# Mixer units 2 to 6 as products of 512 columns over four PSUM banks going round

## The reference, cut to what matters

```python
def short_conv_mixer(h, w_in, conv_w, w_out):
    bg, cg, v = jnp.split(h @ w_in, 3, axis=-1)
    return (bg * causal_dwconv(cg * v, conv_w)) @ w_out
...
x = x + short_conv_mixer(rmsnorm(x, mix_norm[layer]), a_w_in[i], a_conv[i], a_w_out[i])
```

## Time and profile before

| | |
|---|---|
| median of 3 runs | 619.44 us (619.2 to 619.78) |
| the profiled execution's own time | 619.53 us |
| its span, from first to last instruction | 617.8 us |
| TensorE busy | 604.2 us, 98% of the span |
| VectorE busy | 482.2 us, 78% |
| ScalarE busy | 390.6 us, 63% |
| mean granted clock of TensorE | 0.997 |

### The profile page before, as it was taken

The page is one execution under the profiler, slowest core; times in us unless marked ns, Lnnn a source line. Parts: engine busy times, 40 slices in busy tenths (PEclk is TensorE's granted clock), DMA queues, the critical chain, the costliest instruction groups (busy, mean ns, idle before and its releaser), DMA issues.

```text
span 617.8 us, 11378 instructions
## 1 busy us (share of the span) xinstructions
PE 604.2 (98%) x3764; PEld 530.5 (86%) x3764; DVE 482.2 (78%) x955; ACT 390.6 (63%) x727; POOL 57.5 (9%) x81
## 2 busy tenths in 40 slices
PE   9999999999999999999999999999999999999995
PEld 8999997988888888887989877778988888888884
DVE  4888656788888887886877899938788888888765
ACT  7546336766666666667657598737766666666644
POOL 0100011000000000003110156600100000000010
PEclk9999999999999999999999999999999999999998
DMA  8797432355555655781467401023465655555521
GB/s 331 297 342 245 172 136 102 127 214 203 198 198 203 199 199 199 264 288 58 134 205 238 154 2 36 15 94 133 134 213 206 200 194 204 201 191 202 196 102 68
DMA packets 30352, 109.55 MB, mean 177 GB/s; under 512 B 3387, under 2 KB 3659, under 8 KB 30188
## 3 DMA queue, kind: packets, MB, share of 16 engines
q1 hardware_dynamic: 29756, 106.97, 49.4%
q0 software_dynamic: 560, 2.12, 1.0%
HBM read 108.01 MB, written 1.07 MB: 177 GB/s over the span
## 4 chain that ended last, share of the span: by engine, by line
PE 90%; DVE 4%; ACT 2%; issue 1%; DMA 1%; POOL 0%; SPq 0%; DVEq 0%; ACTq 0%
PE bank L1260 24%; PE bank L1264 12%; PE bank L1209 10%; PE bank L1210 10%; PE bank L1211 10%; PE bank L1228 10%; PE bank L1233 5%; PE bank L1305 2%; PE bank L1318 1%; PE bank L1598 1%; DMA bias<-in_xT 1%; DVE work L1132 1%; ACT work L559 1%; PE bank L1555 1%; PE bank L1623 1%
## 5 line engine op out<-in xcount | busy, mean ns | idle before, releaser
L819 DVE TENSOR_TENSOR w<-staged,w 128x1024 fp32r<-128x1024 f32 x188 | 229.2, 1228 | 45.0 <-ACT w L555 44.8
L555 ACT ACTIVATE w<-staged 128x1024 fp32r<-128x1024 f32 x196 | 198.9, 1047 | 21.2 <-PE bank L1211 7.1
L1260 PE MATMUL bank<-gx,w 128*128 128x512 f32 x640 | 159.4, 391 | 0.0
L1260 PEld LDWEIGHTS bank<-gx,w 128*128 128x128 f32 x640 | 117.5, 188 | 23.0 <-DVE work L955 0.2
L1264 PEld LDWEIGHTS bank<-gx,w 128*128 128x128 f32 x640 | 87.3, 190 | 6.2
L1264 PE MATMUL bank<-gx,w 128*128 128x256 f32 x640 | 89.2, 282 | 0.0
L1209 PE MATMUL bank<-w,y 128*128 128x512 f32 x208 | 81.5, 392 | 0.0
L1210 PE MATMUL bank<-w,y 128*128 128x512 f32 x208 | 81.5, 392 | 0.0
L1211 PE MATMUL bank<-w,y 128*128 128x512 f32 x208 | 80.9, 389 | 0.0
L685 ACT ACTIVATE work<-work,params 128x256 f32<-128x256 f32 x96 | 44.2, 504 | 54.0 <-DVE work L955 39.2
L699 ACT ACTIVATE y<-work 128x256 fp32r<-128x256 f32 x52 | 21.7, 418 | 77.8 <-DVE work L976 59.7
(11 more groups left out here) (182 smaller groups left out, 795.8 us busy)
## 6 DMA issues: line engine op xcount, KB each, us to landing
staged<-in_f_up SPq DMA_DIRECT2D x88, 512.0 KB, 5.2
staged<-in_f_down SPq DMA_DIRECT2D x44, 512.0 KB, 3.6
staged<-in_a_up SPq DMA_DIRECT2D x24, 512.0 KB, 7.1
staged<-in_b_up SPq DMA_DIRECT2D x24, 512.0 KB, 4.3
staged<-in_a_down SPq DMA_DIRECT2D x8, 512.0 KB, 3.5
staged<-in_b_down SPq DMA_DIRECT2D x8, 512.0 KB, 4.3
bias<-bias_rows POOLq DMA_DIRECT2D x1, 2048.0 KB, 12.6
x<-in_xt SPq DMA_DIRECT2D x1, 1024.0 KB, 10.0
```

The costliest lines, as they stand in the source:

```text
L555: nc.scalar.activation(w_hi[:, q["slot"], 0:n], staged[:, s, 0:n], ACT.Copy).then_inc(hi, 1)
L819: nc.vector.tensor_tensor(w_lo[:, q["slot"], 0:n], staged[:, s, 0:n], w_hi[:, q["slot"], 0:n].bitcast(F32), ALU.subtract).then_inc(lo, 1)
L1260: nc.tensor.matmul(dst, w_hi[:, s, kt * P:kt * P + P], gx[:, kt, :], start=kt == 0, stop=False, skip_group_check=True)
```

## The change

Units 0, 1 and 7 keep their form (`NARROW` gives their banks). In units 2 to 6 each product has a bank of its own: `w_hi` is multiplied with hi and lo of x at once, in 8 matmuls of 512 columns over the whole bank, and then come the 8 matmuls with `w_lo` over the left half. The left half then holds hi times hi plus lo times hi, the right half hi times lo, and the two halves have to be added. The banks 0 to 3 go round tile after tile (`tile_bank`), so that a bank is used again four tiles later. ScalarE copies the right half into the buffer where the result is to lie, as soon as the product is complete (`lo_read`), and VectorE adds the left half to it (`added`); then VectorE multiplies as before, now from SBUF to SBUF. TensorE waits before each tile for the `added` of the tile that was in its bank. The loops over units are written out.

```diff
+        NARROW = {0: (0, 1), 1: (2, 3), AU - 1: (3, 0)}
+        def tile_bank(k, c):
+            return bank[(3 * (k % 2) + c) % 4]
+        def parts_of(k, c):
+            r = k % 2
+            return {0: shifted[:, r, 1, 2:2 + T], 1: conv[:, r, 1, :], 2: shifted[:, r, 0, 2:2 + T]}[c]
+        def added_of(u, c):
+            return 3 * (u - 2) + c + 1
...
 # ScalarE, step(st, k, ahead, i)
-                for q in early:
-                    lead(*q)
+                if st == "a" and k not in NARROW:
+                    act.wait_ge(y_lo_done["a"], u - 1)
+                    for c in range(3):
+                        if c == 2:
+                            for q in early:
+                                lead(*q)
+                        act.wait_ge(used_up, piece_of("a", "up", k, c)["n"] + 1 + stride("a", "up") * i)
+                        nc.scalar.activation(parts_of(k, c), tile_bank(k, c)[:, T:2 * T], ACT.Copy).then_inc(lo_read["a"], 1)
+                else:
+                    for q in early:
+                        lead(*q)
...
 # VectorE, step(st, k, ahead, i)
-                    nc.vector.tensor_tensor(shifted[:, r, 1, 2:2 + T], bank[2 * r][:, 0:T], rstd[:], ALU.mult)
-                    nc.vector.tensor_tensor(conv[:, r, 1, :], bank[2 * r][:, T:2 * T], rstd2, ALU.mult).then_inc(convolved[st], 1)
-                    dve.wait_ge(convolved[st], 3 * u + 1)
-                    nc.vector.tensor_tensor(shifted[:, r, 0, 2:2 + T], bank[2 * r + 1][:, 0:T], conv[:, r, 1, :],
-                                            ALU.mult).then_inc(scaled[st], 1)
+                    def add(c):
+                        dve.wait_ge(lo_read["a"], added_of(u, c))
+                        nc.vector.tensor_tensor(parts_of(k, c), tile_bank(k, c)[:, 0:T], parts_of(k, c), ALU.add).then_inc(added, 1)
+                        dve.wait_ge(added, added_of(u, c))
+                    add(0)
+                    nc.vector.tensor_tensor(parts_of(k, 0), parts_of(k, 0), rstd[:], ALU.mult)
+                    add(1)
+                    nc.vector.tensor_tensor(parts_of(k, 1), parts_of(k, 1), rstd2, ALU.mult).then_inc(convolved[st], 1)
+                    for q in early:
+                        rest(*q)
+                    early = []
+                    add(2)
+                    dve.wait_ge(convolved[st], 3 * u + 1)
+                    nc.vector.tensor_tensor(parts_of(k, 2), parts_of(k, 2), parts_of(k, 1), ALU.mult).then_inc(scaled[st], 1)
...
 # TensorE, up_a(k, i, cs), units 2 to 6
+                    dst, s, move = tile_bank(k, c), q["slot"], stride("a", "up") * i
+                    if not looped(i) and k == 2:
+                        pe.wait_ge(scaled["a"], 2 if c == 2 else 1)
+                    elif not looped(i) and (k, c) == (3, 0):
+                        pe.wait_ge(scaled["a"], 2)
+                    else:
+                        back, tile = {(0, 0): (1, 1), (0, 1): (1, 2), (0, 2): (2, 2), (1, 0): (2, 0), (1, 1): (1, 0), (1, 2): (1, 1)}[k % 2, c]
+                        pe.wait_ge(added, added_of(u - back, tile))
+                    pe.wait_ge(hi_up, q["n"] + 1 + move)
+                    for kt in range(KT):
+                        nc.tensor.matmul(dst, w_hi[:, s, kt * P:kt * P + P], gx[:, kt, :], start=kt == 0, stop=False, skip_group_check=True)
+                    pe.wait_ge(lo_up, q["n"] + 1 + move)
+                    for kt in range(KT):
+                        mm = nc.tensor.matmul(dst[:, 0:T], w_lo[:, s, kt * P:kt * P + P], gx_hi[:, kt, :], start=False, stop=kt == KT - 1,
+                                              skip_group_check=True)
```

More of the change, by code:

```diff
@@ L241, in build @@
             sem(n) for n in ("rstd_spread", "rstd_ready", "xn_done", "xn_far", "x_turned"))
-        lo_read = {s: sem(f"lo_read_{s}") for s in ("f0", "f1")}
+        lo_read = {s: sem(f"lo_read_{s}") for s in ("a", "f0", "f1")}
+        added = sem("added")
         padded = sem("padded")
@@ L707, in stage @@
                     step(st, 1, AHEAD_A(1))
-                    with act.Fori(0, 2) as i:
-                        for k in (2, 3):
-                            step(st, k, AHEAD_A(k, i), i)
+                    for k in range(2, AU - 2):
+                        step(st, k, AHEAD_A(k))
                     step(st, AU - 2, ([("a", "down", AU - 2, 0)] + nxt[0:1], nxt[1:2], nxt[2:3] + [("a", "down", AU - 1, 0)]))
@@ L942, in step @@
                 early, middle, late = ahead
-                if st == "a":
-                    last = piece_of(st, "up", k, 2)
-                    dve.wait_ge(used_up, last["n"] + 1 + stride(st, "up") * i)
-                    nc.vector.tensor_tensor(shifted[:, r, 1, 2:2 + T], bank[2 * r][:, 0:T], rstd[:], ALU.mult)
-                    nc.vector.tensor_tensor(conv[:, r, 1, :], bank[2 * r][:, T:2 * T], rstd2, ALU.mult).then_inc(convolved[st], 1)
-                    dve.wait_ge(convolved[st], 3 * u + 1)
-                    nc.vector.tensor_tensor(shifted[:, r, 0, 2:2 + T], bank[2 * r + 1][:, 0:T], conv[:, r, 1, :],
-                                            ALU.mult).then_inc(scaled[st], 1)
+                if st == "a" and k in NARROW:
+                    dve.wait_ge(used_up, piece_of(st, "up", k, 2)["n"] + 1)
+                    two, one = (bank[n] for n in NARROW[k])
+                    nc.vector.tensor_tensor(shifted[:, r, 1, 2:2 + T], two[:, 0:T], rstd[:], ALU.mult)
+                    nc.vector.tensor_tensor(conv[:, r, 1, :], two[:, T:2 * T], rstd2, ALU.mult).then_inc(convolved[st], 1)
+                    dve.wait_ge(convolved[st], 3 * u + 1)
+                    nc.vector.tensor_tensor(shifted[:, r, 0, 2:2 + T], one[:, 0:T], conv[:, r, 1, :],
+                                            ALU.mult).then_inc(scaled[st], 1)
+                elif st == "a":
+                    def add(c):
[10 more added lines that the diff above has]
+                    add(2)
+                    dve.wait_ge(convolved[st], 3 * u + 1)
+                    nc.vector.tensor_tensor(parts_of(k, 2), parts_of(k, 2), parts_of(k, 1), ALU.mult).then_inc(scaled[st], 1)
+                if st == "a":
                     halves, per, off = 1, 3, 1
@@ L987, in stage @@
                     step(st, 1, AHEAD_A(1))
-                    with dve.Fori(0, 2) as i:
-                        for k in (2, 3):
-                            step(st, k, AHEAD_A(k, i), i)
+                    for k in range(2, AU - 2):
+                        step(st, k, AHEAD_A(k))
                     step(st, AU - 2, ([("a", "down", AU - 2, 0)] + nxt[0:1], nxt[1:2], nxt[2:3]))
@@ L1243, in up_a @@
             def up_a(k, i=0, cs=range(3)):
-                if k >= 2:
-                    pe.wait_ge(scaled["a"], k - 1 + PER["a"] * i)
+                u = k + PER["a"] * i
                 for c in cs:
-                    fresh = (gx_lo_done, 0) if (k, c) == (0, 0) else (None, None)
-                    dst = bank[2 * (k % 2) + c // 2][:, c % 2 * T:(c % 2 + 1) * T]
-                    product(piece_of("a", "up", k, c), dst, gx_hi, gx_lo, c % 2 == 0, stride("a", "up") * i, *fresh)
+                    q = piece_of("a", "up", k, c)
+                    if k in NARROW:
+                        if k == AU - 1 and c != 1:
+                            pe.wait_ge(added, added_of(*{0: (AU - 3, 0), 2: (AU - 2, 0)}[c]))
+                        dst = bank[NARROW[k][c // 2]][:, c % 2 * T:(c % 2 + 1) * T]
+                        product(q, dst, gx_hi, gx_lo, c % 2 == 0, 0, *((gx_lo_done, 0) if (k, c) == (0, 0) else (None, None)))
+                        continue
+                    dst, s, move = tile_bank(k, c), q["slot"], stride("a", "up") * i
[13 more added lines that the diff above has]
+                                              skip_group_check=True)
+                    mm.then_inc(used_up, 1)
             def up_f(st, k, i=0):
@@ L1431, in stage @@
                     up_a(1, cs=(1, 2))
-                    for k in (2, 3):
+                    for k in range(2, AU):
                         up_a(k)
                         down(st, k - 2)
[L1435 to L1438, removed]
                     last_downs()
```

## The result

The changed kernel takes **624.38 us** (623.82 to 624.61), the kernel before, run beside it, 619.38 (618.92 to 619.99): a ratio of 1.008, with a 95% interval of 1.007 to 1.0091. So it is slower, as forecast, but by 5.0 us instead of 2.5, and outside the range of 620.5 to 623.9. The profiled execution took 624.55.

What follows compares the result with a forecast made beforehand. TensorE, busy 98%, bounds the kernel; 1.5 us won against 3.1 lost in waits leaves 1.6 late, and 0.8 at the tail makes it 2.5 later: 619.53 + 2.5 - 0.09 = 621.9 us, range 620.5 to 623.9 (8 in 10).

Steps and rivals of the forecast that it cites:

- the gain: TensorE, stage a: 15 wide products at 2.78 instead of 2.88 us save 1.5 us; standing alone, 618.0, 1 in 10.
- gap rule: Skill page's gap between matmuls, N / 2.4 + 2.5 ns; by it 15 products would save only 0.3 us.
- The step on VectorE: One step of VectorE's chain after the change, summed from earlier starts: 10.32 us, against 8.86 before.
- both forecast waits on TensorE: TensorE waits for additions: 0.3 us at unit 3's second product, 2.8 us at unit 4's start, until about 51.6.
- the load of down 6: Unit 6's down weights: issued only after unit 5's late `rest`, about 81.3; ScalarE's `lead` begins 3.64 us later, at 85.0.
- Step 2 on VectorE can't start before 40.01: Start of VectorE's chain of additions, held at 40.01 because steps 0, 1 and the loads were taken as untouched.
- the wait in unit 3: TensorE at unit 3's second product, wanted at 40.19, waits for addition (2, 0) at 40.43: 0.3 us lost.
- the longer chain: Rival: VectorE steps of 10.8 us, or a late `lead` or copy on ScalarE, give 623.8; 1 in 10.
- The clock rival: Rival: TensorE's clock halves during the 2.8 us wait, one product costs another 2.8, giving 624.7; 1 in 20.
- my signs of being wrong: Step 3 starting on VectorE before 48, TensorE standing at unit 6 too, or stage a's granted clock below 1.00.
- The tail: End of stage a: TensorE waits 0.8 us for unit 7's `y` at 99.1; last part begins 2.5 us later than before.

Runs made afterwards that it cites:

- e1: Changed kernel with ten unread 512-column matmuls put into TensorE's long wait ahead of unit 4's first product: 624.6 us, ratio 1.0084.
- e2: Changed kernel with GpSimd's 2 MB bias load put off until six additions are made: 622.02 us, ratio 1.0037.
- e8: Changed kernel with early pieces of units 2 to 6 moved behind the third addition, in unit 6 behind the taps; additions start late as before: 623.15 us.
- e10: The kernel of e8 measured once more, unchanged: 622.63 us, ratio 1.0048.
- e11: The kernel of e9 measured once more, unchanged: 621.95 us, ratio 1.004.
- e7: Changed kernel with only the copies and additions of units 2 and 3 moved ahead of the previous unit's late pieces: 620.21 us, ratio 1.0012.
- e4: Changed kernel with both reorderings, units 2 and 3's additions earlier (e7) and early pieces later (e8): 618.42 us, ratio 0.9987.
- e9: The kernel of e8 with ten unread 512-column matmuls filling TensorE's longer wait: 621.86 us, ratio 1.0043.

## Why the prediction was wrong

- **What held.** A product takes 2.79 (forecast 2.78), and the gain was 1.4 of 1.5. The Trainium skill's gap rule ("TensorE: Matmul & The Clock Gate", section "Back-to-back issue gap") would have given 0.3; the rows decide against it. The same section of the Trainium skill calls that rule the gap of an isolated matmul, too low for small ones in a real stream and too high for large ones. The rows agree with the first (120 ns for 256 columns, 109 by the rule) and not with the second: 8 of 512 took 28.03 - 26.19 = 1.84, 230 ns each, against 216. The step on VectorE is 10.40 (10.32), the place and the cause of both forecast waits on TensorE are right, units 5 and 6 wait for nothing. SyncE issued the load of down 6 at 83.29 and its copy began 3.6 later, as forecast.
- **The step that failed: "Step 2 on VectorE can't start before 40.01: everything before it (steps 0 and 1, the loads) is untouched."** I took the start of a chain that the earlier trace rows show waiting for a load as a fixed number. It was 41.58: the load was issued 0.78 later (31.00 for 30.22) and its copy began another 0.8 later behind the issue. All behind it moved along: the wait in unit 3 was 1.31 and not 0.3; unit 4 started at 53.24 and not at 51.6, which is these 1.57 and 0.08 of a longer step. A wait that I didn't have, 0.4 at the third product of unit 2, comes from the same delay of step 1; it cost nothing by itself, since the next products waited for VectorE anyway. On VectorE's chain the same 1.6 and some 0.6 of longer steps give `y` at 101.3, where I had 99.1 (101.7 in e1, where one tap also ran 0.4 longer). That accounts for the miss, as e1 shows, where the clock stays up and the time is the same. e2 takes the load's delay away and measures 622.02. A `lead` that comes late I had named under the longer chain, at 1 in 10 with 623.8, but that number was worked out from longer steps: for the load itself I had no term.
- **The clock rival.** I gave 1 in 20 to a fall in the wait and 624.7 for it, which is near the result, but for another reason. It did fall, which was one of my signs of being wrong, and I had argued from the earlier trace rows, where after the last matmul it was still 1.00 for some 3 us, that 2.8 is short; here it fell after 2.59, and 1.9 sufficed in e2, e8 and e10. One reading of an idle stretch doesn't bound it. Its price was 1.7 and not 2.8, since by the windows above it lasted from about 54.3 to 57.8, 3.4 us at half rate; and in the changed kernel it lay beside VectorE's lateness. Only where the tail was shortened (e8 against e11) did it reach the end of the stage. The same page of the Trainium skill, in its part on the HAM clock gate, has idleness halve the clock and work give it back; the windows above agree.
- **The tail.** Forecast: 0.8 of wait at the end. In the changed kernel none is seen, because TensorE itself was late; in e1 and e7 it is there with 1.4. The order of the late work was right and the size too small; 0.4 of the 1.4 is a slow tap whose cause is open.
- **The sum with what was measured**: 4.79 after unit 7's end at 96.85 is 101.64, against 96.65: 4.99 late, and 619.53 + 4.99 = 624.5, the profiled 624.55. Nothing behind the mixer moved by itself.

## What to carry to other kernels

Where a change uses up slack, every number on the path that fed the slack becomes part of the sum, and a start that a load sets needs a range of its own. Repeating the profile of the kernel before would not have given it here: three of them have the copy at 37.78 to 37.93, while the profiles of the changed kernels have it anywhere from 38.07 to 39.46, and at 36.80 with the 2 MB put off. A wait that the change makes is first a question of order: moving the operations that free a bank ahead of those that wait for a load, and those that only prepare later work behind them, turned 5.0 us of loss into 1.0 of gain with the same instructions. When two chains end within a few tenths, an edit to one shows nothing (e1); shorten the other as well, and its price comes out (e8 against e11, and e4, which mends both).

## What the runs showed of the hardware

- The granted clock fell to 0.50 after idle stretches of 1.9 to 2.6 us on TensorE (e2, e8, e10, the changed kernel twice), and not after those of 1.3 to 1.6 in unit 3 (the changed kernel, e8, e1), though in the stretch after the program's last matmul it held longer. The fall came only once TensorE was at work again, and cost 1.7 us in each of these five profiles. Ten matmuls of 512 columns (2.4 us) in the gap kept it at 1.00 (e1, e9, e11).
- Two loads on different queues share the DMA engines: with the 2 MB of GpSimd under way, the 512 KB of down 1 were used 7.6 to 8.6 us behind their issue; where they took longer (8.0 to 8.6), the 2 MB took less (11.0 to 11.8 for 11.9 to 12.6). With that load put off, the copy began at 36.80, 6.1 behind the issue, without having waited for the load.
